# A distance of its own, by a fixed rule, for every slot of a weight ring in SBUF

## Time and profile before

| What | us |
|---|---|
| median of 2 timed runs | 1481.11 (1480.06 to 1482.16) |
| the profiled execution's own time | 1483.28 |
| its span, first to last instruction | 1481.5 |
| mean granted TensorE clock, share of full speed | 0.998 |

### The profile page before, as it was taken

The page is one execution under the profiler, slowest core; times in us unless marked ns, Lnnn a source line. Parts: engine busy times, 40 slices in busy tenths (PEclk is TensorE's granted clock), DMA queues, the critical chain, the costliest instruction groups (busy, mean ns, idle before and its releaser), DMA issues.

```text
span 1481.5 us, 23028 instructions
## 1 busy us (share of the span) xinstructions
PE 1468.4 (99%) x9666; PEld 1307.8 (88%) x9666; DVE 1160.6 (78%) x1534; ACT 793.7 (54%) x995; POOL 39.3 (3%) x41
## 2 busy tenths in 40 slices
PE   8999999999999999999999999999999999999999
PEld 7888898888988888888889878799999998989978
DVE  7987776787898865988658678779998899666844
ACT  6444456565454443544445566555545645675653
POOL 0000001210000000000001110000000000000000
PEclk9999999999999999999999999999999999999999
DMA  8655545444455555555554444465555453335541
GB/s 320 209 190 196 179 170 198 144 149 165 171 201 180 197 177 201 190 190 187 191 192 155 172 171 143 171 208 196 204 192 192 154 196 131 127 107 182 181 142 57
DMA packets 38390, 262.18 MB, mean 177 GB/s; under 512 B 4624, under 2 KB 5008, under 8 KB 8464
## 3 DMA queue, kind: packets, MB, share of 16 engines
q1 hardware_dynamic: 38144, 260.72, 50.4%
q10 hardware_dynamic: 144, 0.00, 0.0%
HBM read 259.66 MB, written 1.05 MB: 176 GB/s over the span
## 4 chain that ended last, share of the span: by engine, by line
PE 91%; DVE 7%; ACT 1%; issue 1%; DMA 0%; SPq 0%; ACTq 0%
PE ps L301 21%; PE ps L238 13%; PE ps L240 13%; PE ps L239 13%; PE ps L308 10%; PE ps L797 8%; PE ps L802 4%; DVE w_low L223 3%; PE ps L326 1%; PE ps L1543 1%; PE ps L328 1%; DVE scratch L2246 1%; PE ps L1534 0%; PE ps L1516 0%; DMA setup_first<-in_first 0%
## 5 line engine op out<-in xcount | busy, mean ns | idle before, releaser
L223 DVE TENSOR_TENSOR w_low<-w_raw,w_high 128x2048 fp32r<-128x2048 f32 (+2 forms) x244 | 551.6, 2262 | 149.8 <-ACT w_high L217 147.8
L217 ACT ACTIVATE w_high<-w_raw 128x2048 fp32r<-128x2048 f32 (+2 forms) x244 | 460.2, 1887 | 370.3 <-PE ps L308 168.5
L301 PE MATMUL ps<-x,w_high 128*128 128x512 f32 x1328 | 317.7, 392 | 0.0
L301 PEld LDWEIGHTS ps<-x,w_high 128*128 128x128 f32 x1328 | 243.4, 188 | 47.6
L308 PEld LDWEIGHTS ps<-x,w_low 128*128 128x128 f32 x1328 | 167.1, 188 | 7.0
L308 PE MATMUL ps<-x,w_low 128*128 128x256 f32 x1328 | 169.2, 280 | 0.0
L238 PE MATMUL ps<-w_high,x 128*128 128x512 f32 (+1 forms) x448 | 166.4, 372 | 0.0
L240 PE MATMUL ps<-w_high,x 128*128 128x512 f32 (+1 forms) x448 | 161.7, 361 | 0.0
L239 PE MATMUL ps<-w_low,x 128*128 128x512 f32 (+1 forms) x448 | 161.5, 361 | 0.0
L238 PE MATMUL ps<-x,w_high 128*128 128x256 f32 x456 | 129.4, 284 | 0.5 <-DVE x L364 0.5
L797 PE MATMUL ps<-ffn_hid,w_high 128*128 128x512 f32 x528 | 127.8, 392 | 0.0
(11 more groups left out here) (477 smaller groups left out, 2332.5 us busy)
## 6 DMA issues: line engine op xcount, KB each, us to landing
w_raw<-in_weights SPq DMA_DIRECT2D x231, 1024.0 KB, 4.9
w_raw<-in_weights SPq DMA_DIRECT2D x10, 768.0 KB, 4.3
w_raw<-in_weights SPq DMA_DIRECT2D x5, 512.0 KB, 4.0
even_second_vectors<-in_second SPq DMA_DIRECT2D x1, 1836.0 KB, 7.4
setup_first<-in_first SPq DMA_DIRECT2D x3, 512.0 KB, 6.6
resid<-in_x SPq DMA_DIRECT2D x1, 1024.0 KB, 10.2
out<-resid SPq DMA_DIRECT2D x3, 256.0 KB, 2.2
table<-in_table SPq DMA_DIRECT2D x1, 737.0 KB, 8.2
```

The costliest lines, as they stand in the source:

```text
L217: act.activation(self.slot(self.wh, n), self.slot(self.raw, n), ACT.Copy).then_inc(self.hi_made, 1)
L223: dve.tensor_tensor(self.slot(self.wl, n), self.slot(self.raw, n), self.slot(self.wh, n).bitcast(F32), ALU.subtract).then_inc(self.lo_made, 1)
L301: pe.matmul(c.bank(bank + i).rearrange("p (a t) -> p a t", a=2), wh[:, k, i * P:(i + 1) * P], c.x[:, :, k, :], start=(k == 0), stop=False, ...
```

## The change

The lists of offsets are made by a rule in place of one constant per kind of slot. Slots 0 and 1 of each feed-forward part lie at distance 0, high and low. Every other slot n of a feed-forward part takes its two distances, one for high and one for low, from a list of 16: multiples of 32 in parts 0 and 2 (in the other order in part 2), odd multiples of 16 in part 1, and sixteen small distances, many of them no multiple of 16, in part 3. In the mixers, the even and the odd layer, high and low share a distance, and it steps through the multiples of 32. No instruction, size, wait or transfer changes.

```diff
-WIDE, THREE, LOWS, SQUARE, FULL = 16, -64, 32, -32, 0
-DOWN = (*range(4, LAST_DOWN, 3), LAST_DOWN)
-FF_HIGH = [LINE] + [below(WIDE)] * (FF_SLOTS - 1)
-FF_LOW = [LINE] + [below(LOWS)] * (FF_SLOTS - 1)
-LAST_HIGH = [below(THREE) if n in DOWN else FF_HIGH[n] for n in range(FF_SLOTS)]
-LAST_LOW = [below(THREE) if n in DOWN else FF_LOW[n] for n in range(FF_SLOTS)]
-MIX_AT = [below(FULL if S_DV <= n < S_POOL or S_GATE <= n < S_OUT else THREE) for n in range(MIX_SLOTS)]
-EVEN_AT = [below(THREE if n < A_Q or n >= A_GLU else SQUARE if n < A_V else FULL) for n in range(EVEN_SLOTS)]
-ODD_AT = [below(FULL if G_V <= n < G_OUT else THREE) for n in range(ODD_SLOTS)]
-HIGH_AT = (FF_HIGH + MIX_AT + FF_HIGH) * (DEPTH - 1) + FF_HIGH + MIX_AT + LAST_HIGH + EVEN_AT + ODD_AT
-LOW_AT = (FF_LOW + MIX_AT + FF_LOW) * (DEPTH - 1) + FF_LOW + MIX_AT + LAST_LOW + EVEN_AT + ODD_AT
+def ffn_at(part):
+    high = [LINE, LINE] + [below(STEPS[part][5 * n % 16]) for n in range(2, FF_SLOTS)]
+    low = [LINE, LINE] + [below(STEPS[part][(11 * n + n // 16 * 5 + 3) % 16]) for n in range(2, FF_SLOTS)]
+    return high, low
+
+
+EVENS = [32 * i for i in range(16)]
+ODDS = [32 * i + 16 for i in range(16)]
+FINE = [4, 8, 12, 20, 24, 28, 36, 40, 60, 68, -4, -8, -12, -20, -56, -72]
+STEPS = [EVENS, ODDS, EVENS[::-1], FINE]
+FFNS = [ffn_at(part) for part in range(2 * DEPTH)]
+MIXERS = [[below(32 * (5 * n + layer) % 512) for n in range(MIX_SLOTS)] for layer in range(DEPTH)]
+REST = [below(32 * (7 * n) % 512) for n in range(EVEN_SLOTS + ODD_SLOTS)]
+HIGH_AT = FFNS[0][0] + MIXERS[0] + FFNS[1][0] + FFNS[2][0] + MIXERS[1] + FFNS[3][0] + REST
+LOW_AT = FFNS[0][1] + MIXERS[0] + FFNS[1][1] + FFNS[2][1] + MIXERS[1] + FFNS[3][1] + REST
 LOW_AT[1] = LINE
```

## The result

The changed kernel takes 1501.88 us (median of 2 runs, 1501.8 to 1501.95) where the kernel before takes 1481.11: a ratio of 1.0139, 95% interval 1.0122 to 1.0155. The forecast was 1499, with a range from 1484 to 1520.

The account below looks back on a forecast made before the run. TensorE, busy 1468.4 of 1481.5 us, was taken as the bound. Terms 7.3 + 0 + 5.6 + 5.0 = 17.9 us on the profiled 1483.3 gave 1501.2, less 2.2 for the median: 1499 us, range 1484 to 1520.

Parts of the forecast that it names:

- a pitch counts one for one: Whole kernel: no wait is left to win, so anything that alters a TensorE matmul pitch alters the time equally.
- The two ports of the Trainium skill: TensorE has independent read ports, so addresses cannot matter: worth 0, 1481 us; chance 0.20 together with distances averaging out.
- Kind A: 1856 feed-forward matmuls on high slots, 512 columns in two pieces, distance 16: 7.3 us more, bounds -3.9 to +18.6.
- The ranking of the parts: Line 301 worse in parts 0 and 2 (5 ns more) than part 1 (2 ns); part 3 was given 4 ns.
- Kind B: 1856 feed-forward matmuls on low slots, 256 columns, distance 32: 0 us, bounds -6.9 to +5.6.
- Kind C: 3288 matmuls of 256 columns in threes, line 238: states redrawn at each slot, 5.6 us more, bounds -6.6 to +14.8.
- Kind D: 1260 matmuls of 512 columns in one piece, distance 0: 4 ns more each, 5.0 us, bounds -2.5 to +11.3.
- A new start at each slot: About 125 slots of Kind C and Kind D would newly pay an unsettled start: at most 5 us, counted within them.
- The splits at nothing: Lines 223 and 217, writing w_low and w_high at other offsets, were costed at nothing.
- Averages out: Rival: a run's state depends on its start, not distance; 1481 to 1486, say 1484 us; 0.20 together with two ports.
- The other way: Rival: most distances are better than 16 and 32, runs settle at the floors; -20 us, 1461 us; chance 0.07.
- Collide throughout: Rival: weight load and stream read the same memory part all slot long; 1511 to 1531, say 1518 us; chance 0.24.

Follow-up runs that it names:

- both maps: Kernel before with the feed-forward low slots' distance stepping through 64 multiples of 4 bytes, high at 16 or at 0; one execution each, 1486.54 and 1484.62 us.
- the last one: Kernel before with low slots and Kind C at 180, queries and keys of the even layer at 64, high at 16, Kind D at 0; 1475.25 us, ratio 0.9946.

## Why the prediction was right, and where it was not

**What bounds the kernel, and that a pitch counts one for one.** Right in the main: TensorE is busy for 99% after as before, and the time rose with its pitches. The pitches of the four kinds cost 24.5 us. What was left out is that a slower TensorE also waits less: of the 5.8 us that did not reach the span, 2.3 are the lower clock in the profiled execution of before, and some 3.5 are waits and other pitches outside the table. That busy time and median both rose by 21 us (20.9 and 20.8) is partly chance, as the spans of the same two executions differ by 18.7.

**The two ports of the Trainium skill.** By the page "TensorE: Matmul & The Clock Gate" of the Trainium skill (Part 2, step by step) there would have been no difference. Moving the rows by 64 bytes, the slots staying, cost 1.55%; the traces disagree. The formula that this page of the Trainium skill gives for the gap of matmuls without their weight loads ("Back-to-back issue gap") works out, as an estimate, to 215.8 ns for 512 columns and 109.2 for 256 at 2.4 GHz; here, with a weight load for each matmul, the lowest settled pitches at the upper level are 226.7 and 113.3.

**Kind A, 7.3 us, measured 5.9.** The size was near, the reasoning was not. The step "the only multiple of 32 seen with this form is 0, with 6 ns more" took the alternating matmuls of slot 0 for a measurement of the distance. At 0 kind A is at its floor (391 ns in the run with all distances 0). The other multiples of 32 are what costs: in the changed kernel 233.4 ns at 32, 233.3 at 96, 234.2 at 160 (and 228.9 at 64, in six of seven slots). The ranking of the parts was wrong as well: parts 0 to 3 lost 3.4, 3.1, 3.3 and 3.6 ns in line 301, so odd multiples of 16 (2 ns forecast) were hardly better than multiples of 32 (5 ns forecast). That the sum came near is luck.

**Kind B, 0 us, measured 3.0.** The step "in the middle of what 256 columns show" failed: 116.7 was on the low side. The mean over the distances is 118.4 to 118.5 settled, as the changed kernel and both maps show.

**Kind C, 5.6 us, measured 10.4.** Half of the mechanism held: before, 2039 of the 2903 matmuls with rows streaming lay in runs in the 113 ns state, the mean was 115.0, and new distances took them out of it. But the step "that state is drawn again at every slot" was not what happened. With 256 bytes added at every second slot the states stayed (0.5 us less); in the changed kernel 96 of the 2903 settle at 113, and the rest between 115 and 121, most of them at 118 to 120. So the mean went to 118.2, not to the middle of floor and ceiling, and the term was half of what it should have been.

**Kind D, 5.0 us, measured 5.2.** Right in size, 4 ns chosen from 0 to 12 where 4.4 were measured, and so in part luck. The nearest row, that of kind A, was the right one: in the changed kernel the two have nearly the same settled pitches at 32 (233.3) and at 0 (226.6 to 230.2 for D, mostly 226.7 for A). At 64 and 192 they are swapped: A has 228.9 ns at 64 and about 233 at 192, D 233.1 to 233.5 at 64 and about 229 at 192, with one slot of each out of line. As D streams the weights and A the rows, this is what one map of the streaming minus the stationary address would give; no run was made to test it.

**A new start at each slot.** Bounded at 5 us and counted in C and D. No run shows the term. The first six matmuls of a slot of kind D (the 40 slots with the rows x) cost 15.1 ns more in all than six settled ones before, 15.0 with 256 added at every second slot, and 2.3 in the changed kernel, where the settled pitch is higher: no new start was paid for either a new address or a new distance.

**The splits at nothing.** Right, 2297 ns before and after.

**The rivals.** "Averages out" had its grain of truth, two states at one distance (worth 2.3 us where rows and slots moved together), but falls with the run of the moved rows. "The other way" was wrong as a forecast of this change, and right that most of kinds A and B stood above the floor: one number in one line took 0.4% off. "Collide throughout" has its place in single distances only: the pitch over 245 ns, named as what would prove me wrong, exists, at distance 100, which the change did not use for kind A.

The total of 17.9 us against 20.8 came out close partly by luck, by errors of both signs: A 1.4 too much, B 3.0 and C 4.8 too little, and nothing for what came back.

## What to carry to other kernels

In this kernel, bound by TensorE with float32r data, the address of the stationary tile relative to the streaming rows, modulo 256 bytes, is worth 2% of the time (1474.3 to 1506.4 us from the best median to the worst), and 16 columns more in an unrelated buffer moved it by 1.55%. Elsewhere that is to be measured. Read the busy column or the starts, not the mean duration, and compare a form at one distance with the same form in the same order; a matmul in an alternating sequence says nothing about one in a run of its own kind. A kernel that steps the distance over its slots gives the whole map in one execution; it should visit each distance after different ones, or its repeats test little. And compare timed runs with the same granted clock, where the record has it, before a difference under 0.5% is read.

## What the runs showed of the hardware that I had not expected

**A period of 256 bytes and a floor of 17/16.** Adding 256 at every second slot changes no kind by more than 0.5 us. The lowest settled pitches, 113.3 and 226.7 ns, are 272 and 544 cycles at 2.4 GHz, 16 for every 256 columns above the column count.

**At the lower level of the clock the penalty is gone**, at the two distances where it was seen (-32 and 64, queries and keys). In the kernel before, TensorE waits in the even layer until the matmuls of line 2409 start. Timeline, start us and us:

```profile
1250.79 0.28 PE L240 MATMUL ps<-w_high,x 128*128 128x256 f32 x1
1253.08 0.46 PE L2409 MATMUL ps<-even_u,even_b_c 128*128 128x128 f32 x2 [2.00 <-DVE even_u L2256]
```

The stretch behind it, in the kernel before, then in the one with C at 180, then in the last one (columns as in the earlier trace rows):

```profile
1250.00:1262.00 12.00, 9.99 (x89) 9.28 (x87) 11.69 (x20) 3.61 (x10) 0.00 (x0) 0.72 0.46 162
```

```profile
1244.00:1256.00 12.00, 10.47 (x117) 9.85 (x116) 11.69 (x21) 4.31 (x12) 0.00 (x0) 1.00 0.47 160
```

```profile
1247.00:1259.00 12.00, 9.80 (x74) 8.90 (x75) 11.69 (x22) 3.59 (x10) 0.00 (x0) 0.58 0.47 165
```

The granted clock falls to a mean of 0.72 and 0.58, that is, for part of the stretch to the level of 1.2 GHz, after a wait of 2.3 us (start 1250.79 to start 1253.08) in the first and of 2.5 us in the third; it stays at 1.00 in the second, where the wait was 1.8 us. The length of the wait does not decide it alone. With the low slots at 180 the wait was as long as before, 2.3 us (start 1245.15 to start 1247.44), and the clock stayed up:

```profile
1246.00:1258.00 12.00, 10.56 (x124) 9.90 (x125) 11.71 (x21) 5.46 (x18) 0.00 (x0) 1.00 0.52 174
```

At the lower level a matmul of 256 columns takes 213 ns from start to start, which is 256 cycles at 1.2 GHz and not one more. The run of 24 costs 2.3 to 2.4 us, with smaller matmuls beside it more. What makes an execution fall there was not tried, but the clock of the timed runs goes with their spread: of the twelve runs of the kernel before that stand beside the one with the low slots at 180, the three at 1.000 took 1480.04 to 1480.68 us and the four at 0.996 or 0.997 took 1484.22 to 1485.31.

What stays open: why a distance has the pitch that it has. The runs show the map, not the mechanism, and not what chooses between two states at one distance. A constant distance of 136 for kind A, whose starts are cheaper than those at 16 (230, 230, 230 against 233, 239, 232 ns), wasn't tried.
